# A two-layer decoder step on one core: the order of layer 1's attention blocks, who scales their outputs, one maximum over both maps, and three smaller moves

## The reference, cut to what matters

```python
def block(xs):
    qblk, i = xs
    ...
    bias = jnp.where(dist >= 0, -slopes[:, None, None] * dist, -jnp.inf)
    p1 = jax.nn.softmax(jnp.einsum('bqhd,bkhd->bhqk', qf[..., :DH_B], k1) + bias, axis=-1)
    p2 = jax.nn.softmax(jnp.einsum('bqhd,bkhd->bhqk', qf[..., DH_B:], k2) + bias, axis=-1)
    return jnp.einsum('bhqk,bkhv->bqhv', p1 - lam * p2, vf)
```

## Time and profile before

| | us |
|---|---|
| three timed runs, median | 2049.24 |
| lowest, highest | 2048.81, 2052.35 |
| the profiled execution | 2054.24 |
| its span | 2052.4 |
| TensorE busy in the span | 1583.4 (77%) |
| VectorE busy | 753.0 (37%) |
| ScalarE busy | 390.5 (19%) |
| GpSimd busy | 364.8 (18%) |
| mean granted TensorE clock, of full speed | 0.865 |
| HBM traffic | 274 GB/s |

### The profile page before, as it was taken

The page is one execution under the profiler, slowest core; times in us unless marked ns, Lnnn a source line. Parts: engine busy times, 40 slices in busy tenths (PEclk is TensorE's granted clock), DMA queues, the critical chain, the costliest instruction groups (busy, mean ns, idle before and its releaser), DMA issues. The chain is left out here.

```text
span 2052.4 us, 22129 instructions
## 1 busy us (share of the span) xinstructions
PE 1583.4 (77%) x7466; PEld 729.2 (36%) x7467; DVE 753.0 (37%) x1314; ACT 390.5 (19%) x755; POOL 364.8 (18%) x274
## 2 busy tenths in 40 slices
PE   6999976786288998946889887777495399989950
PEld 2333335233133333312346563344342233333320
DVE  1010134575400000036755568995455400000008
ACT  1010022011022122222120002333211011222212
POOL 0000000001010000023735566650001000000004
PEclk8989987588589999977999998889796599999985
DMA  8652620611589989969969999884402579999972
GB/s 330 256 198 84 245 84 12 229 71 52 238 329 428 376 352 425 427 275 328 362 225 378 405 389 411 336 319 139 185 21 82 224 291 386 409 428 428 428 296 92
DMA packets 122909, 563.03 MB, mean 274 GB/s; under 512 B 13621, under 2 KB 43126, under 8 KB 101307
## 3 DMA queue, kind: packets, MB, share of 16 engines
q1 hardware_dynamic: 98450, 496.63, 61.0%
q10 hardware_dynamic: 15424, 33.08, 4.2%
q0 software_dynamic: 8944, 32.15, 4.2%
HBM read 521.80 MB, written 40.03 MB: 274 GB/s over the span
## 5 line engine op out<-in xcount | busy, mean ns | idle before, releaser
L1488 PE MATMUL ps<-arena_w,arena_r 128*64 128x512 f32 x1664 | 378.6, 612 | 33.5 <-issue 28.5
L1488 PEld LDWEIGHTS ps<-arena_w,arena_r 128*64 128x64 f32 x1664 | 126.4, 141 | 279.4 <-issue 273.3
L1470 PE MATMUL ps<-arena_w,arena_r 128*64 128x512 f32 x832 | 186.9, 597 | 19.2 <-ACT arena_r L1518 19.2
L1565 DVE TENSOR_TENSOR arena_r<-arena_r,ps 128x512 f32<-128x512 f32 x38 | 26.2, 688 | 441.9 <-ACT arena_r L1535 441.9
L1868 POOL TENSOR_TENSOR arena_w<-arena_w,arena_r 128x1024 f32<-128x1024 f32 x48 | 116.4, 2430 | 112.5 <-DMA arena_w<-in_cache_k_dram 111.9
L1921 PE MATMUL ps<-arena_w,xt 128*128 128x256 f32 x512 | 124.3, 405 | 1.4 <-ACT xt L2086 1.4
L1868 POOL TENSOR_TENSOR arena_r<-arena_r 128x1024 f32<-128x1024 f32 x48 | 115.0, 2400 | 48.9 <-DMA arena_r<-in_cache_k_dram 48.8
L512 PE MATMUL ps<-arena_w,xt 128*128 128x512 f32 x256 | 113.6, 601 | 0.4 <-PE ps L206 0.4
L1091 POOL TENSOR_TENSOR x_res<-x_res,arena_m 128x1024 f32<-128x1024 f32 (+1 forms) x20 | 52.6, 2631 | 341.6 <-DVE x_res L1085 341.6
L1022 PE MATMUL ps<-arena_w,xt 128*128 128x512 f32 x256 | 111.1, 593 | 0.0
L1921 PEld LDWEIGHTS ps<-arena_w,xt 128*128 128x128 f32 x512 | 103.0, 204 | 18.2 <-ACT xt L2086 1.5
(11 more groups left out here) (355 smaller groups left out, 1959.1 us busy)
## 6 DMA issues: line engine op xcount, KB each, us to landing
arena_w<-in_w_exp_gate_dram SPq DMA_DIRECT2D x38, 2048.0 KB, 13.4
arena_w<-in_w_exp_up_dram SPq DMA_DIRECT2D x38, 2048.0 KB, 17.2
arena_w<-in_w_exp_down_dram SPq DMA_DIRECT2D x38, 2048.0 KB, 18.9
arena_m<-in_cache_v_dram SPq DMA_DIRECT2D x128, 512.0 KB, 8.3
arena_w<-in_cache_k_dram SPq DMA_DIRECT2D x64, 512.0 KB, 8.3
arena_r<-in_cache_k_dram SPq DMA_DIRECT2D x64, 512.0 KB, 9.8
arena_w<-in_w_ada_dram SPq DMA_DIRECT2D x12, 2048.0 KB, 16.8
arena_m<-in_w_ada_dram SPq DMA_DIRECT2D x12, 2048.0 KB, 8.5
```

The lines of the kernel that those rows point to most:

```text
L1470: last = nc.tensor.matmul(psy[c][at:at + 64, :], ht[u][:, k, 64 * (1 - a):64 * (2 - a)], wd[u][:, k, c * 512:(c + 1) * 512], start=(k == 0 ...
L1488: last = nc.tensor.matmul(ps[at:at + 64, :], xgt[u][:, k, 64 * a:64 * (a + 1)], w[u][:, k, :], start=(k == 0), stop=(k == KT - 1), tile_po ...
```

## The change

- Layer 0, sample part: the selector and the sample rows' values each have a second copy on partitions 32 to 39. The second half of a spread product uses the copy, in another row group of the array. ScalarE makes one more 8 x 512 copy for it, GpSimd fills and selects twice, and the semaphore counts each product.
- Decoder, blocks: `finish` is cut in `turn(u)` and `finish(u)`. TensorE's order becomes turn(u - 2), scores(u), values, finish(u - 2). ScalarE's becomes c_copy(u - 2), second_weight(u - 1), powers(u), keep(u - 3).
- `keep` goes from VectorE to ScalarE, as an activation with the scale `r1`. VectorE gets a wait that guards `r1`.
- The two maximum instructions of a block become one over both maps.
- The four later pieces of own-row weights are started from ScalarE's queue, each behind the copy of the product that frees its buffer, and not from SyncE's.
- The load of a new value row moves by one group.

```diff
@@ stage_gla_project, scalar
                 s.wait_ge(sm_mm, c + 1)
+                if c == 1:
+                    nc.scalar.copy(m.v[32:32 + NS, NTT - 1, 512:1024], m.ps[1][0:NS, :])
@@ stage_gla_sample
-    sel = m.R[0:NS, off + 32 + HA * NS * NS:off + 32 + HA * NS * NS + NS * P]
+    sel = [m.R[32 * n:32 * n + NS, off + 32 + HA * NS * NS:off + 32 + HA * NS * NS + NS * P] for n in range(2)]
...
-                v.wait_ge(vb_mm, b + 1)
+                v.wait_ge(vb_mm, 2 * b + 2)
...
-                    last = nc.tensor.matmul(m.ps[2 * (b % 2) + n][:, :], sel[:, b * P:(b + 1) * P],
-                                            m.v[0:NS, NTT - 1, n * 512:(n + 1) * 512], start=True, stop=True)
-                last.then_inc(vb_mm, 1)
+                    nc.tensor.matmul(m.ps[2 * (b % 2) + n][:, :], sel[n][:, b * P:(b + 1) * P],
+                                     m.v[32 * n:32 * n + NS, NTT - 1, n * 512:(n + 1) * 512], start=True, stop=True,
+                                     tile_position=(32 * n, 0)).then_inc(vb_mm, 1)
@@ stage_decoder, sync
-            for c in range(QCH):
-                sp.wait_ge(sp_mm, QCH + c + 1)
-                sp.dma_start(own_w[c], dec.source(a, 2 * QCH + c)).then_inc(mk_in[c], 16)
...
-                if g >= LAG and (g - LAG) % 4 == 1:
+                if g >= LAG and (g - LAG) % 4 == 2:
@@ stage_decoder, tensor
-            def finish(u):
-                h, i = u // NQ, u % NQ
+            def turn(u):
+                i = u % NQ
                 pe.wait_ge(dl_ok, u + 1)
                 wait(pe, c_cp, u)
...
                 last.then_inc(c_tr, 1)
+
+            def finish(u):
+                h, i = u // NQ, u % NQ
                 pe.wait_ge(c_cp, u + 1)
                 wait(pe, o_ev, u)
...
                 for n, u in enumerate(dec.units(g)):
+                    if u >= dec.DEPTH:
+                        turn(u - dec.DEPTH)
                     scores(u)
...
                         for late in range(u - dec.DEPTH + 1, u + 1):
+                            turn(late)
                             finish(late)
@@ stage_decoder, scalar
                 nc.scalar.copy(shares[c % 2], OWN[c % 2][:, 0:CW]).then_inc(spa_cp, 1)
+                if c < 2 * QCH:
+                    s.dma_start(own_w[c - QCH], dec.source(a, c + QCH)).then_inc(mk_in[c - QCH], 16)
...
+            def keep(u):
+                h, i = u // NQ, u % NQ
+                s.wait_ge(o_mm, u + 1)
+                s.wait_ge(r_ok, u + 1)
+                nc.scalar.activation(m.v[:, i, h * DVB:(h + 1) * DVB], O_B[:, (u % 2) * DVB:(u % 2 + 1) * DVB], ACT.Copy,
+                                     scale=r1[i]).then_inc(o_ev, 1)
...
+                    if u >= dec.DEPTH:
+                        c_copy(u - dec.DEPTH)
                     if u:
                         second_weight(u - 1)
-                    if u >= dec.DEPTH:
-                        c_copy(u - dec.DEPTH)
                     powers(u)
+                    if u > dec.DEPTH:
+                        keep(u - dec.DEPTH - 1)
...
                     if u == NQ * HB - 1:
                         second_weight(u)
+                        keep(u - dec.DEPTH)
                         for late in range(u - dec.DEPTH + 1, u + 1):
                             c_copy(late)
+                            keep(late)
@@ stage_decoder, vector
-                V.reciprocal(r1[u % NQ], ls[u % NB][:, 0:1])
-
-            def keep(u):
...
+                if u >= NQ:
+                    v.wait_ge(o_ev, u - NQ + 1)
+                V.reciprocal(r1[u % NQ], ls[u % NB][:, 0:1]).then_inc(r_ok, 1)
...
-                for j in range(2):
-                    last = V.tensor_reduce(out=mx[u % NB][:, j:j + 1], in_=SP[u % NB][j][:, 0:w], axis=AX.X, op=ALU.max, negate=True)
-                last.then_inc(nb_ok, 1)
+                V.tensor_reduce(out=mx[u % NB], in_=view(m.W, 1024 * (u % NB), 2, 512)[:, :, 0:w], axis=AX.X, op=ALU.max,
+                                negate=True).then_inc(nb_ok, 1)
...
-                if u > dec.DEPTH:
-                    keep(u - dec.DEPTH - 1)
                 block_scores(u)
```

More of the change, by code:

```diff
@@ L845, in _ @@
         def _(g):
[L847 to L851, removed]
+            for n in range(2):
+                nc.gpsimd.memset(sel[n], 0.0).then_inc(sel_ok, 1)
+            for n in range(2):
+                g.wait_ge(sel_ok, n + 1)
+                blocks = sel[n].rearrange("r (b n) -> r b n", n=P)
+                nc.gpsimd.affine_select(out=blocks, in_=blocks, compare_op=ALU.not_equal, fill=1.0, base=0,
+                                        pattern=[[-1, NS], [0, P]], channel_multiplier=1).then_inc(dg_ok, 1)
         @block.scalar
@@ L879, in _ @@
         def _(pe):
-            pe.wait_ge(dg_ok, 1)
+            pe.wait_ge(dg_ok, 2)
             pe.wait_ge(qs_ok, 1)
@@ L1727, in stage_decoder @@
          "om_ok", "or_mm", "or_ev"))
-    k_tr, kt_ok, sc_mm, sb_ok, nb_ok, p_ok, c_ok, dl_ok, c_tr, c_cp, o_mm, o_ev = (sem(n) for n in
-        ("k_tr", "kt_ok", "sc_mm", "sb_ok", "nb_ok", "p_ok", "c_ok", "dl_ok", "c_tr", "c_cp", "o_mm", "o_ev"))
+    k_tr, kt_ok, sc_mm, sb_ok, nb_ok, p_ok, c_ok, r_ok, dl_ok, c_tr, c_cp, o_mm, o_ev = (sem(n) for n in
+        ("k_tr", "kt_ok", "sc_mm", "sb_ok", "nb_ok", "p_ok", "c_ok", "r_ok", "dl_ok", "c_tr", "c_cp", "o_mm", "o_ev"))
     kk, vv, qt = view(m.W, 8192, NQ, D), view(m.W, 12288, NQ, D), view(m.W, 16384, HB, SEQ)
@@ L1763, in stage_decoder @@
     lm = [m.small[:, 52 + i:53 + i] for i in range(2)]
+    rinv = m.small[:, 54:55]
     col = m.small[:, 64:96].rearrange("p (v k) -> p v k", k=KT)
@@ L2292, in weigh @@
                 v.wait_ge(p_ok, u + 1)
[L2293 removed]
+                V.reciprocal(rinv, ls[u % NB][:, 1:2])
                 v.drain()
[L2295 removed]
+                V.tensor_scalar(lm[u % 2], ls[u % NB][:, 0:1], rinv, neg_lam, ALU.mult, ALU.mult).then_inc(c_ok, 1)
                 v.drain()
[L2297 to L2303 removed]
+                if u >= NQ:
+                    v.wait_ge(o_ev, u - NQ + 1)
+                V.reciprocal(r1[u % NQ], ls[u % NB][:, 0:1]).then_inc(r_ok, 1)
             def block_scores(u):
@@ L2326, in attend @@
                     weigh(u)
-                    for late in range(u - dec.DEPTH, u + 1):
-                        keep(late)
             v.wait_ge(pad_ok, 1)
@@ L2401, in _ @@
             v.drain()
+            v.wait_ge(o_ev, NQ * HB)
             V.memset(m.xt[:, :, TOK:SEQ + 32], 0.0)
```

6 lines of the change are left out of this document (removed).

## The result

The changed kernel takes **2087.01 us** (median of four runs, 2079.0 to 2088.3), where the kernel before took 2050.8 beside it. The ratio is 1.0161, with a 95% interval of 1.0137 to 1.0184: slower, as forecast, but by 33 us (1.6%) and not by 10, and outside the range that I gave. (The two medians lie 36 us apart.

A forecast was written before the change was run, and what follows sets the result against it. TensorE was taken to bound layer 0's sample part, VectorE the decoder blocks with pages, hand-overs the tail. Terms -8 - 4 - 1 + 13 + 11.5 - 1.7 = +9.8 us gave 2059.0 us, range 2038 to 2076.

The forecast's parts named there:

- The circle: Decoder attention blocks: scores, VectorE's work, powers, scaling, value product, next turn, next scores become strictly serial; +13 and +11.5 us.
- Check 1: Decoder blocks: TensorE's value product waits for ScalarE's scaling, mostly behind powers, in nearly each block.
- check 2: Tail blocks: VectorE's first add waits for scores in nearly each block, for tens of us in all.
- the decoder's start: Decoder before the blocks: moved own-row weight loads give -4 us (0 to -9), later value-row load -1 (0 to -2.5).
- check 5: Decoder: the first value page comes about 4 us nearer to the stage's start.
- Check 4: Layer 0, sample part: a sequence takes 3.1 to 3.4 us.
- From there to 1290 us the stage goes by the DMA engines: Decoder up to 1290 us: transfers set the pace and an earlier start is carried through; blocks 0 to 3 cost 0.
- the two terms of the circle: Blocks 4 to 21, with pages: +13 us (5 to 20); tail from block 22: +11.5 us (8 to 16).
- Check 3: Decoder tail: scores of blocks 22 to 31 lie some 57 us apart.
- The cover holds: Blocks with page sums: the moved scaling gates nothing there, so that stretch saves 6 us; 2040 us, chance 0.20.
- No overlap: Layer 0, sample part: the row pair doesn't overlap with 8 rows, so 8 us are not gained; 2067 us, chance 0.08.
- The clock falls further: Decoder blocks: TensorE's idling brings more time at the low clock, +10 us over 27 blocks; 2069 us, chance 0.14.

The follow-up runs named there:

- needless products: Changed kernel plus 4 to 10 unread 128 x 128 products a block on TensorE: 2078.59 us, ratio 1.0131; run again 2073.44 us, ratio 1.0082.

## Why the prediction was off

**Right: the mechanism and the sign.** The circle is there, through the steps named. Check 1 holds (26 of 32 blocks, behind powers), check 2 holds (28.4 us of VectorE's waits in the tail alone, 69.7 in all), and moving the scaling from behind powers to the head of its step removes 51 us.

**Right: the decoder's start, but less sure than the table looks.** -5 was forecast, and in the profile scores(0) come 5.1 us nearer to the stage's start. That row scatters: it is 282.5 to 288.3 us in the fourteen profiles with the new start, and 287 to 289 in the three with the old one. The runs of this part alone give 3.5 us (0 to 7). What doesn't overlap is check 5, the first value page, at 89.5 to 91 us and at 93 to 94: from the stage's first load to it before took 1053.7 - 959.8 = 93.9 us, and the changed kernel 1037.6 - 947.6 = 90.0 (L1796 is the stage's first load; the first number behind "ns" that isn't a duration is the first start):

```profile
L1796 SPq DMA_DIRECT2D small<-in_page_table_dram x1: 255/255/255, 947.6 to 947.6; - x1
...
L1816 SPq FUSED_REGOPS  x128: 37/37/37, 1037.6 to 1483.1; - x128
```

**Size a little off: layer 0.** Forecast -8, measured -10.7 in the profile and -8.8 (4 to 13) in the runs of this part alone. The term that was too large is the 3.25 us of a sequence. The pair of spread products took 2.08 us where the sum had 2.2 (the 512-column pair of scores at the lower level takes 2.08 as well, in the row at 1444.63). TensorE goes from pair to pair in 2.98 us, where the sum had 3.1, and the 0.15 on top for hand-overs wasn't needed: the spread runs ahead, and VectorE goes without a wait, 2.78 us from one multiply-add to the next:

```profile
362.92 2.08 PE L892 MATMUL ps<-arena_w,arena_r 8*128 8x512 f32 x4
363.01 1.66 DVE L874 SCALAR_TENSOR_TENSOR arena_w<-ps,arena_w 128x256 f32<-128x256 f32 x4
...
365.80 1.66 DVE L874 SCALAR_TENSOR_TENSOR arena_w<-ps,arena_w 128x256 f32<-128x256 f32 x4
...
368.58 1.66 DVE L874 SCALAR_TENSOR_TENSOR arena_w<-ps,arena_w 128x256 f32<-128x256 f32 x4
```

Check 4 (3.1 to 3.4 us a sequence) was thus missed: the sequence is shorter. The Trainium skill's page TensorEngine Tiling (Theoretical Speedup) gives a factor of up to 2 for two row tiles; here it was 3.78 / 2.08 = 1.8, and VectorE sets the pace, as it would by that rule.

**Too large by the runs: the parts in front together.** The sum had -13 for them. The kernel with both and nothing else gained 8.0 us (4 to 12). Of the 23 us between the forecast of +9.8 and the +33 measured, that is 5, and the blocks are the other 18.

**Failed: "From there to 1290 us the stage goes by the DMA engines".** I costed the circle at nothing for blocks 0 to 3, because the transfers fill that stretch. They do, before and after (share 1.03). But the circle is there as well, and takes longer than in the tail, since page work lies in it. This is the changed kernel, from scores(3) to the value product of block 1:

```profile
1256.34 3.04 DVE L2250 TENSOR_TENSOR arena_r<-arena_r 128x1024 f32<-128x1024 f32 x1
...
1256.53 1.13 PE L1991 MATMUL ps<-xt,arena_w 64*128 64x512 f32 x4
...
1261.12 1.41 DVE L2329 SCALAR_TENSOR_TENSOR arena_w<-arena_r,small,ps 128x512 f32<-128x512 f32 x2
...
1265.30 0.35 ACT L2153 ACTIVATE arena_w<-ps,small 128x128 f32<-128x128 f32 x1
...
1265.79 1.19 PE L2010 MATMUL ps<-arena_w,xt 128*128 128x128 f32 x4 [8.13 <-ACT arena_w L2153]
```

TensorE stands still for 8.13 us, while VectorE works on pages ahead of the block. The four blocks took 38.8 and 38.5 us. In the four profiles with unchanged blocks they took 28.6 to 29.9 (mean 29.5): +9 where the sum had 0. With the needless products they took 33.0 and 34.6, so part of the 9 seems to come by the clock as well. Not all of it need be the circle's: in the seven kernels below without it, whose blocks differ from before's, these blocks took 26.7 to 34.2 us. Counted from the stage's first load, block 4 comes at 322.3 and 321.0 us in the changed kernel and at 312.9 to 317.4 in the nine kernels with the new start and no circle, so the loss is 4 to 9 us. Nor was it the transfers that came late. Up to 320 us behind the stage's start the DMA engines are as full in the changed kernel as in the same kernel with the scaling first; in the next 10 us (1268 to 1278 in both traces) their share is 0.77 with the circle and 1.03 without. The blocks fall behind while the transfers are still full, and the transfers thin out 10 us earlier.

**Mis-sized: the two terms of the circle, by the clock.** Against the mean of the four profiles with unchanged blocks (119.1 and 48.9 us), the stretch with pages costs +18.6 (forecast +13) and the tail +18.9 (forecast +11.5). Raised to a clock of 0.93 to 0.96, the stretches took 130.0 and 61.9 us (means of two profiles), or +10.9 and +13.0. Against this stand my prices at the high clock: 4.5 rounds x 2.0 = +9, and 10.1 + 1.4 = +11.5. By this count both prices were right within 2 us. It sets a raised clock against before's own, though. Against the kernel with the scaling first and the same products (111.2 and 50.0 us, at 0.97 and 1.00) the circle costs 18.8 and 11.9 us: the tail's price stands by both counts, that of the stretch with pages by one only, and it stays open which is the fairer, since the scaling first also saves VectorE's time. What was too small by either count is the allowance for the clock. In the stretch with pages I added 4 us on the clock of before (0.86), less than my own working: +2.0 and +1.5 a round make 3.5, and the sum took 2.9, some 3 us less in all. In the tail I added nothing, and put a further fall of the clock among the rivals with 0.14. In the traces the fall comes with the circle: 0.83 and 0.78 from block 4 on, and 8 + 6 us, by what the needless products gave back. As both are one mechanism, the rival belonged into the sum. The forecast priced TensorE's idle time as time, and not also as a lower level of the clock for the work around it.

The Trainium skill (TensorE: Matmul & The Clock Gate, HAM oscillation) warns that idle gaps return the array to half rate. The prediction cited that and left the sum as it was; the trace bears the page out, with the clock falling from 0.93 to 0.78 in the tail.

**Check 3** (scores 22 to 31 some 57 us apart) failed with 67.8 us, for the same reason; at 0.96 it is 61.6 and 62.1. **The end** was -0.6 and not -1.7: the tail of the unchanged kernels varies as much (22.6 to 25.4 us), so I don't read more into it. The saved maximum is as priced: one instruction at 512 columns takes 1.22 us, where the two took 1.28 together.

**The rivals.** "The cover holds" (2040) is refuted by VectorE's waits. "No overlap" of the row pair is refuted by 2.08 us. "The clock falls further" (2069) was the right one beside the forecast, and still 18 us short: 4 to 9 us for the first four blocks, some 5 for the parts in front, and the rest in the size of the clock's term.

**Left open:** executions of one kernel differ by up to 20 us (2037.1 to 2057.3 with layer 0's part alone), and the two profiles of the kernel with needless products differ by 6 us in the stretch with pages at clocks of 0.96 and 0.93; I don't know what sets that. The value product waits for every earlier scaling though its output goes to the other half of the bank. Waiting for one less would cut the circle as well, but then one engine writes a PSUM bank that another reads, unordered; it wasn't tried.

## What to carry to other kernels

When a step moves to another engine, its place in that engine's queue counts for more than its price: a scaling of 0.35 us behind a step that waits for the next block cost some 50 us more than the same scaling at the head of the step. Write the queue orders side by side, and look for a circle that leads from an instruction through the waits to the same instruction of the next round; if there is one, the sum of its parts is the time of a round. A circle that leaves TensorE idle is to be priced twice, at the high clock and at the level that the idle time brings.

## What I had not expected of the hardware

- Needless products shortened the kernel: 4 to 10 more a block took the granted clock from 0.83 and 0.78 to 0.93 to 0.96, and 6 to 16 us off the whole. In a kernel without the circle the same products raised it from 0.88 and 0.89 to 0.97 and 1.00 and neither cost nor gained anything (0.9909 against 0.9913).
- Unchanged code, nine blocks long, took 47.4 to 48.1 us at a granted clock of 0.90 to 0.94 in three profiles, and 52.1 us at 0.83 in a fourth.
- Two fp32 products with only 8 rows each, 512 columns wide, in different row groups of the array, took 2.08 us where they had taken 3.78, both in a stretch at the lower clock level (0.54 and 0.53).
